# Sixteen modulation tiles of a hybrid layer: from split products on 128 stationary columns to plain fp32 products on four column groups

## The chip, the core and the metric

The kernel runs on one core of a Trainium2 chip. The metric is the device time of one execution in microseconds (us): the median of several runs, and, for the reading, one execution recorded by the hardware profiler.

## What is computed

One layer of a diffusion backbone works on 1280 tokens (1024 latent, 256 context) of width 1024 in fp32: norm, modulation, one input projection, attention beside a bidirectional scan, output projection, feed-forward. The part that matters here is the modulation (adaLN):

```python
def adaln(cond, w_mod, b_mod):
    m = jax.nn.silu(cond) @ w_mod + b_mod      # cond: 1024 values, w_mod: 1024 x 6144
    return jnp.split(m, 6, axis=-1)            # shift, scale, gate (mixer), shift, scale, gate (FFN)
```

It is called for two vectors, `c` (latent tokens) and `c_ctx` (context tokens), with the same `w_mod`. So it is a product of a 2 x 1024 matrix with a 1024 x 6144 matrix: much weight, and only two rows of result.

## The kernel before, in words

`w_mod` is cut into 24 tiles of 256 columns (`MOD_W`), each 1024 x 256: 1 MB, held as 128 partitions x 8 k-pieces x 256. The first eight (`FirstMod`, L229) are computed at the start, while the first data arrive, and are not touched by the change. The other sixteen (`ModStage`, L307), numbered n = 0 to 15 here (tile 8 + n of the 24), run between the tiles of the input projection.

**Numbers.** Nearly all products of the kernel are "split" ones: a value is written as hi + lo, both in the format fp32r, and TensorE multiplies hi by hi, hi by lo and lo by hi (`split3`, L407; lines L409 to L411 of the profile are these three for all such products). For a modulation tile ScalarE copies the tile rounded into `hi` (`act_hi`, L342, 128 x 2048 elements), VectorE subtracts to get `lo` (`dve_lo`, L348). The stationary operand `cond_st` has 128 columns: 32 copies of hi and 32 of lo of the first vector, then the same of the second. The product (`pe_product`, L354) is 16 matmuls for one tile: 8 k-pieces, each with `hi` and with `lo` as the moving operand of 256 columns, all added up in one PSUM tile of 128 x 256, `psM`. VectorE copies `psM` into `row` (`dve_row`, L366). Then `pe_turn` (L373) multiplies with a 0/1 matrix of two columns, `K_SUM`, that adds row 0 and row 32 of each half. For a gate tile (n = 0 to 3 and 12 to 15) the 0/1 matrix is the stationary operand (2 columns) and the moving one has 256 columns (L380); for the other eight the row is stationary (128 columns, two of them) and the moving operand has 2 columns (L383). Both are in plain fp32. `dve_col` (L387) takes the result out of PSUM, and GpSimd's queue stores the gate rows.

**Order.** `SEQUENCE` (L52) is the hand-written order of the input projection: 14 projection tiles with smaller steps (fold, cache, sums) among them. A projection tile is 72 split matmuls in three token blocks. `mod_step(n)` on TensorE is `pe_turn(n - 1)` and then `pe_product(n)`. `MODS` (L58) gives its places: n = 0 before the first smaller step, n = 1 to 6 each behind one projection tile, 7 to 14 two for each of the tiles 8 to 11 (one in the middle of the tile, one behind it), 15 in the middle of tile 12. On ScalarE and VectorE `act_hi` and `dve_lo` stand at places of the same list (`at_start`, `after`, `ahead`), among the splits of the projection weights, the convolutions of the xbc tiles and the evictions.

**Buffers.** The weight tiles go through a ring of two (`m2_wring`), loaded by SP's queue in order with the projection weights; the load of tile n waits until `dve_lo` of tile n - 2 is done (L337). `hi`, `lo` and `psM` have one slot each. Later the place of the ring and of `hi`/`lo` is used for the z weights: ScalarE's split of the first of these waits for the last `dve_lo` (L763), VectorE's for the last modulation product (L954).

Of the kernel before, what the change touches and what calls it, by code (L numbers as in the profile page):

```python
# [23 lines left out]
P = 128  # L24
F32 = mybir.dt.float32
# [7 lines left out]
KD = D // P  # L33
# [37 lines left out]
C_GPRE, C_GFFN, C_BMOD, C_GQ, C_GKV, C_CW, C_CB, C_GS, C_DB, C_AL, C_DS = 0, 8, 16, 64, 67, 69, 93, 101, 105, 121, 137  # L71
N_COLS = 141

K_ID, K_MASK, K_SEL, K_FOLD, K_TRI, K_SA, K_SB, K_MT, K_MD, K_SUM = 0, 128, 384, 400, 528, 656, 672, 672, 688, 704
N_CONST = 706


class Chain:
# [58 lines left out]
def across(ap, n):  # L137

    p, a = ap.shape
    return ap.unsqueeze(2).to_broadcast([p, a, n])  # L140
# [166 lines left out]
class ModStage:  # L307

    def __init__(self, L, st, tag, first, last, banks, depth, slots):
        self.L, self.first, self.last, self.banks, self.depth, self.slots = L, first, last, banks, depth, slots
        self.ring = L.sb(st, f"{tag}_wring", [P, depth, KD, MOD_W])
        self.hi, self.lo = (L.sb(st, f"{tag}_w_{n}", [P, slots, KD, MOD_W], F32R) for n in ("hi", "lo"))
        self.row = L.sb(st, f"{tag}_row", [P, MOD_W])
        self.gate = L.sb(st, f"{tag}_gate", [2, 2, MOD_W])
        self.psM = L.ps(st, f"{tag}_psM", [P, banks, 512])
        self.psC = L.ps(st, f"{tag}_psC", [P, 512])
        self.loaded = [L.sem(f"{tag}_w_loaded{i}") for i in range(depth)]  # L320
        self.row_out = [L.own_sem(f"{tag}_row_out{i}") for i in range(2)]
        self.hi_ready, self.lo_ready, self.product, self.row_ready, self.turned, self.col_ready = (
            L.sem(f"{tag}_{n}") for n in ("w_hi", "w_lo", "product", "row_ready", "turned", "col_ready"))

    @staticmethod
    def is_gate(j):
# [6 lines left out]
    def load(self, eng, j):  # L333
        i = j - self.first
        r = i % self.depth
        if i >= self.depth:
            eng.wait_ge(self.lo_ready, i + 1 - self.depth)  # L337
        eng.dma_start(flat(self.ring[:, r, :, :]), self.L.dram["w_mod"][j]).then_inc(self.loaded[r], 16)

    def act_hi(self, act, j):  # L340
        i = j - self.first
        r = i % self.depth  # L342
        act.wait_ge(self.loaded[r], 16 * (i // self.depth + 1))
        if i >= self.slots:
            act.wait_ge(self.product, i + 1 - self.slots)
        act.activation(self.hi[:, i % self.slots, :, :], self.ring[:, r, :, :], ACT.Copy).then_inc(self.hi_ready, 1)

    def dve_lo(self, dve, j):  # L348
        i = j - self.first
        dve.wait_ge(self.hi_ready, i + 1)  # L350
        dve.tensor_tensor(self.lo[:, i % self.slots, :, :], self.ring[:, i % self.depth, :, :],
                          self.hi[:, i % self.slots, :, :].bitcast(F32), ALU.subtract).then_inc(self.lo_ready, 1)

    def pe_product(self, pe, j):  # L354
        i = j - self.first
        pe.wait_ge(self.lo_ready, i + 1)
        if i >= self.banks:
            pe.wait_ge(self.row_ready, i + 1 - self.banks)
        for k in range(KD):
            for w in (self.hi, self.lo):  # L360
                mm = pe.matmul(self.psM[:, i % self.banks, :MOD_W], self.L.cond_st[:, k, :],
                               w[:, i % self.slots, k, :], start=(k == 0 and w is self.hi),
                               stop=(k == KD - 1 and w is self.lo))
        mm.then_inc(self.product, 1)

    def dve_row(self, dve, j):  # L366
# [6 lines left out]
    def pe_turn(self, pe, j):  # L373
        i = j - self.first
        pe.wait_ge(self.row_ready, i + 1)
        if i >= 1:
            pe.wait_ge(self.col_ready, i)
        total = self.L.const[:, K_SUM:K_SUM + 2]
        if self.is_gate(j):
            mm = pe.matmul(self.psC[0:2, :MOD_W], total, self.row[:], start=True, stop=True)  # L380
        else:
            for s in range(2):
                mm = pe.matmul(self.psC[:, 2 * s:2 * s + 2], self.row[:, s * P:(s + 1) * P], total, start=True,  # L383
                               stop=True)
        mm.then_inc(self.turned, 1)
# [36 lines left out]
def phase_front(L):  # L422
# [6 lines left out]
    with ExitStack() as st:  # L429
# [19 lines left out]
        def at(name, home, skip, shape, dt=F32):  # L449
# [37 lines left out]
        staged = at("w_mod_staged", "hT_hi", 0, [P, 2, KD, T])  # L487
        spare_hi, spare_lo = (at(f"m1_w_{n}", "m2_wring", i * KD * MOD_W * 4, [P, KD, MOD_W], F32R)
                              for i, n in enumerate(("hi", "lo")))
        first_rows = at("m1_rows", "m2_row", 0, [P, 2, MOD_W])  # L490
        first = FirstMod(L, lambda k: staged[:, :, k, 0:KD // 2 * MOD_W], (mod.hi[:, 0, :, :], spare_hi[:]),
                         (mod.lo[:, 0, :, :], spare_lo[:]), (mod.psM[:, 0, :], psP[:, 0, 1, :]), mod.psC, first_rows)
# [61 lines left out]
        after = lambda m: MODS.get(number.get(m), ())[len(midway(m)):]  # L554
        splits = lambda m: SPLIT_AT.get(number.get(m), ())
        for_tile = lambda ct: ct < N_TILES

        def ahead(m):

            return midway(m + 1 + (SEQUENCE[m + 1][0] == "sumq")) if m + 1 < len(SEQUENCE) else ()  # L560

        def at_start(m):

            before = [i for i in range(m) if SEQUENCE[i][0] == "xbc" and ahead(i) == midway(m)]
            return () if before else midway(m)


        down = list(range(NT_LAT - 1, -1, -1)) + list(range(NT - 1, NT_LAT - 1, -1))
# [187 lines left out]
        def _(act):  # L756
            chain = Chain(act, ach)

            def split(ct):
                act.wait_ge(loaded[ct % 2], 16 * (ct // 2 + 1))  # L760
                if not for_tile(ct):
                    n = ct - N_TILES
                    act.wait_ge(mod.lo_ready, last_mod)  # L763
                    act.activation(flat(wz_hi[:, 2 * n:2 * n + 2, :]), flat(raw[:, ct % 2, :, :]), ACT.Copy
                                   ).then_inc(hi_ready, 1)
                    return
                if ct >= 2:
                    until(act, tiles[ct - 2])
                act.activation(w_hi[:, ct % 2, :, :], raw[:, ct % 2, :, :], ACT.Copy).then_inc(hi_ready, 1)
# [15 lines left out]
            for n in range(3 * KD):  # L785
# [2 lines left out]
                    split(1)  # L788
                if n in X_LATER:
                    norm.act_square(act, X_LATER[n])  # L790
            mod.act_hi(act, MOD_EARLY)
            act.wait_ge(ip_consts, 3)
            for m, (kind, i) in enumerate(SEQUENCE):
                for ct in splits(m)[:1]:
                    split(ct)
                for n in at_start(m):
                    mod.act_hi(act, MOD_EARLY + n)
                for ct in splits(m)[1:]:
                    split(ct)
                for n in after(m):  # L800
                    if n >= 1:
                        mod.act_hi(act, MOD_EARLY + n)
                src = flat(bank(m))[:, 0:T]
                if kind == "rope":
                    until(act, m)
# [1 line left out]
                    act.activation(conv[64:128, :], src[0:64, :], ACT.Copy).then_inc(swapped, 1)  # L807
                    act.activation(dt_raw[64:80, :], src[64:80, :], ACT.Copy).then_inc(dt_copied, 1)
                if kind == "xbc":
                    for n in ahead(m):  # L810
                        mod.act_hi(act, MOD_EARLY + n)
                    n = xbc_order.index(i)
                    act.wait_ge(conv_ready, n + 1)
                    if i >= 6:
                        act.wait_ge(kv_stored, 16)
                        until(act, place["out", 0])
                    elif i == 0:
                        until(act, place["sumq", 0])
                    elif i == 2:
                        act.wait_ge(qn_ready, KQ)  # L820
                    elif i == 3:
                        act.wait_ge(q_stored, 16)
                    act.activation(L.xbcT[:, i, :], conv[:], ACT.Silu,
                                   bias=L.cols[:, C_CB + i:C_CB + i + 1]).then_inc(conv_read, 1)
                    continue
# [121 lines left out]
        def _(dve):  # L947
# [101 lines left out]
            for n in range(3 * KD):  # L1049
# [5 lines left out]
                    norm.dve_mean(dve, X_LATER[n])  # L1055
                if n - 1 in X_LATER:
                    norm.dve_scale(dve, X_LATER[n - 1])
            mod.dve_lo(dve, MOD_EARLY)
            dve.wait_ge(turn.h_ready, 24)
            for m, (kind, i) in enumerate(SEQUENCE):  # L1060
                for n in splits(m)[:1]:
                    split(n)
                for n in at_start(m):
                    mod.dve_lo(dve, MOD_EARLY + n)
                for n in midway(m):
                    mod.dve_col(dve, MOD_EARLY + columns(m)[0])
                    mod.dve_row(dve, MOD_EARLY + n)
                for n in splits(m)[1:]:
                    split(n)
                for n in after(m):  # L1070
                    if n >= 1:
                        mod.dve_lo(dve, MOD_EARLY + n)
                src = flat(bank(m))
                if kind == "rope":
                    dve.wait_ge(t_loaded, 32)
# [53 lines left out]
                for n in columns(m)[-1:]:  # L1129
                    mod.dve_col(dve, MOD_EARLY + n)  # L1130
                if kind == "xbc":
                    for n in ahead(m):
                        mod.dve_lo(dve, MOD_EARLY + n)
                    if SEQUENCE[m - 1][0] == "sumq":
                        normalise(KQ, 3, C_GQ, qn_ready)
                if kind == "kv" and i == 1:
# [86 lines left out]
        def _(pe):  # L1223
# [54 lines left out]
            for n in range(2 * KD - 2, 3 * KD):  # L1278
                first_tiles(n, (1,))
            pe.wait_ge(turn.modulated, 3 * KD)  # L1280
            mod_step(0)
            for m, (kind, i) in enumerate(SEQUENCE):
                if m < 2:
# [1962 lines left out]
def shape_constants(np):  # L3246
# [8 lines left out]
    const[:, K_FOLD:K_FOLD + P] = (i % 64) == (j % 64)  # L3255
    const[:, K_TRI:K_TRI + P] = i <= j
    const[:, K_SUM:K_SUM + 2] = (i % 32 == 0) & (i // 64 == np.arange(2)[None, :])
    forward = np.arange(16) < SH
    const[:, K_SA:K_SA + 16] = np.where(forward, 1.0, -1.0)
    const[:, K_SB:K_SB + 16] = np.where(forward, 0.0, 1.0)  # L3260
# [92 lines left out]
```

## Time and profile before

| | |
|---|---|
| median of 3 runs | 1720.67 us (1719.91 to 1720.94) |
| profiled execution, first to last instruction (span) | 1720.2 us |
| TensorE (PE) busy | 1661.6 us, 97% |
| VectorE (DVE) busy | 1041.4 us, 61% |
| ScalarE (ACT) busy | 726.0 us, 42% |
| granted TensorE clock, mean | 0.993 of full |

The profiled execution is known by its span alone; its own time beside it is not listed. Its span lies 0.5 us under the median of the runs and inside their range. In the timeline views each row is one instruction (or several of the same kind in sequence, with their count): start in us, length in us, engine, line, operation, output <- inputs, rows*columns of the stationary operand and the shape of the moving one; in brackets the idle time of the engine before it and what ended it. Matmuls are pipelined, so their lengths overlap: the time that one takes from the engine is the distance to the next start, not its length. PEld is the load of the stationary operand, which runs ahead of the matmul. DVEq is an event on VectorE's queue that comes with no work of its own.

### The profile page before, as it was taken

The page shows a single profiled execution, that of the slowest core. Times are in us where ns is not written, and L with a number is a line of the kernel's source. Part 1 is how long each engine was busy: PE and PEld are TensorE (multiplying, and loading weights), DVE is VectorE, ACT ScalarE, POOL GpSimd, SP SyncE. Part 2 cuts the span into 40 slices and gives each one's busy share as a digit, 9 for nine tenths or more (in the row PEclk, how much of TensorE's full clock was granted, in tenths as well). Part 3 has the DMA queues.
Part 4 walks back from the last instruction along what each step waited for, and adds up shares of the span by engine and source line. Part 5 has one row for each costly group of instructions (what it writes and reads, how often), then busy time and mean ns, then how long its engine had stood idle before and what let it go on. Part 6 is the DMA issues. An engine that isn't in the chain of part 4 may idle for free. (4 is left out here: it accounts for less than half of the span.)

```text
span 1720.2 us, 24950 instructions
## 1 busy us (share of the span) xinstructions
PE 1661.6 (97%) x9786; PEld 1488.8 (87%) x9795; DVE 1041.4 (61%) x1590; ACT 726.0 (42%) x1213; POOL 79.7 (5%) x116
## 2 busy tenths in 40 slices
PE   5999999999899999999999999999999999999998
PEld 5788888878778888887888999999999999888886
DVE  5856765338765555474578554555455545467788
ACT  5753332334544544464565333333333333434453
POOL 0110000014200000000100000000000000000011
PEclk9999999999999999999999999999999999999999
DMA  9234342012400000114321221222222224773455
GB/s 372 80 135 145 117 146 89 11 34 65 114 13 19 1 14 1 69 37 157 131 86 50 103 103 72 88 95 96 88 79 103 92 83 163 247 231 98 124 164 186
DMA packets 76292, 176.35 MB, mean 103 GB/s; under 512 B 10353, under 2 KB 26945, under 8 KB 74129
## 3 DMA queue, kind: packets, MB, share of 16 engines
q1 hardware_dynamic: 72080, 169.75, 28.6%
q0 software_dynamic: 4096, 5.01, 0.9%
q8 instruction: 79, 1.29, 0.3%
q14 instruction: 37, 0.30, 0.1%
HBM read 131.02 MB, written 43.70 MB: 102 GB/s over the span
## 5 line engine op out<-in xcount | busy, mean ns | idle before, releaser
L409 PE MATMUL psF<-gv,gu_ring 128*128 128x320 f32 x1224 | 379.3, 310 | 3.8 <-DVE gv L2714 3.1
L411 PE MATMUL psF<-gv,gu_ring 128*128 128x320 f32 x1224 | 378.9, 310 | 0.0
L410 PE MATMUL psF<-gv,gu_ring 128*128 128x320 f32 x1224 | 378.8, 310 | 0.0
L409 PEld LDWEIGHTS psF<-gv,gu_ring 128*128 128x128 f32 x1224 | 230.4, 188 | 4.7 <-issue 3.6
L410 PEld LDWEIGHTS psF<-gv,gu_ring 128*128 128x128 f32 x1224 | 230.4, 188 | 0.0
L411 PEld LDWEIGHTS psF<-gv,gu_ring 128*128 128x128 f32 x1224 | 230.4, 188 | 0.0
L409 PE MATMUL psF<-d_w_ring,d_hid_ring 128*128 128x512 f32 x360 | 140.2, 389 | 0.0
L410 PE MATMUL psF<-d_w_ring,d_hid_ring 128*128 128x512 f32 x360 | 140.1, 389 | 0.0
L411 PE MATMUL psF<-d_w_ring,d_hid_ring 128*128 128x512 f32 x360 | 140.1, 389 | 0.0
L409 PE MATMUL psP<-hT_hi,win_hi 128*128 128x512 f32 (+1 forms) x336 | 122.2, 364 | 2.3 <-DVE hT_lo L184 1.6
L2514 ACT ACTIVATE hraw<-psF 128x320 f32<-128x320 f32 x130 | 56.7, 438 | 149.8 <-PE psF L411 148.5
L411 PE MATMUL psP<-hT_hi,win_lo 128*128 128x512 f32 (+1 forms) x336 | 119.3, 355 | 0.0
L410 PE MATMUL psP<-hT_lo,win_hi 128*128 128x512 f32 (+1 forms) x336 | 119.2, 355 | 0.0
L2764 DVE TENSOR_TENSOR hraw<-hraw,psF 128x320 f32<-128x320 f32 x132 | 63.4, 485 | 41.1 <-ACT hraw L2514 35.1
L1843 DVE TENSOR_TENSOR pt_lo<-psPT,pt_hi 128x512 fp32r<-128x512 f32 (+1 forms) x104 | 58.3, 582 | 41.0 <-ACT pt_hi L1719 41.0
L2556 ACT ACTIVATE d_hid_ring<-d_hid 128x640 fp32r<-128x640 f32 x54 | 40.0, 740 | 98.5 <-PE psF L411 95.4
L2510 ACT ACTIVATE gu_ring<-raw_gu 128x512 fp32r<-128x512 f32 x65 | 40.9, 629 | 96.1 <-PE psF L411 96.1
L409 PEld LDWEIGHTS psF<-d_w_ring,d_hid_ring 128*128 128x128 f32 x360 | 67.6, 188 | 14.5 <-DVE hraw L2953 0.5
L411 PEld LDWEIGHTS psF<-d_w_ring,d_hid_ring 128*128 128x128 f32 x360 | 67.6, 188 | 14.1
L410 PEld LDWEIGHTS psF<-d_w_ring,d_hid_ring 128*128 128x128 f32 x360 | 67.6, 188 | 13.8
L2821 DVE TENSOR_TENSOR d_hid_ring<-d_hid,d_hid_ring 128x640 fp32r<-128x640 f32 x54 | 44.5, 824 | 53.8 <-ACT d_hid_ring L2556 53.6
L1719 ACT ACTIVATE pt_hi<-psPT 128x512 fp32r<-128x512 f32 (+1 forms) x104 | 52.2, 515 | 54.8 <-PE psPT L1985 53.6
(447 smaller groups left out, 3640.5 us busy)
## 6 DMA issues: line engine op xcount, KB each, us to landing
hid_variants<-hraw SPq DMA_DIRECT2D x77, 320.0 KB, 2.2
d_hid<-hid_variants SPq DMA_DIRECT2D x58, 320.0 KB, 3.0
m_wring<-in_w_mod SPq DMA_DIRECT2D x16, 1024.0 KB, 4.9
d_b<-in_w_down SPq DMA_DIRECT2D x44, 256.0 KB, 4.2
win_raw<-in_w_in SPq DMA_DIRECT2D x18, 512.0 KB, 5.4
w_mod_staged<-in_w_mod SPq DMA_DIRECT2D x16, 512.0 KB, 11.8
d_hid_more<-hid_variants SPq DMA_DIRECT2D x19, 320.0 KB, 3.0
raw_gu<-in_w_gate SPq DMA_DIRECT2D x11, 512.0 KB, 3.8
```

The costliest lines, as they stand in the source:

```text
L409: pe.matmul(out, w_hi, x_hi, start=first, stop=False, skip_group_check=onto)
L410: pe.matmul(out, w_hi, x_lo, start=False, stop=False, skip_group_check=onto)
L411: return pe.matmul(out, w_lo, x_hi, start=False, stop=last, skip_group_check=onto)
L1719: act.activation(pt_hi[:, g[0]:g[-1] + 1, r:r + P], psPT[:, (g0 + i) % 2, 0:len(g), :], ACT.Copy).then_inc(pth_ready, 1)
L1843: dve.tensor_tensor(pt_lo[:, g[0]:g[-1] + 1, r:r + P], psPT[:, (g0 + i) % 2, 0:len(g), :], pt_hi[:, g[0]:g[-1] + 1, r:r + P].bitcast(F32), ...
L2510: act.activation(w_slot(q)[:, 0, :], block_of(r, n), ACT.Copy).then_inc(wv_hi, 1)
L2514: act.activation(dst[:, chunk(c)], psA(n, c), ACT.Copy).then_inc(copied, 1)
L2556: act.activation(ring_h(e, 0), hr[e % HR], ACT.Copy).then_inc(h_hi, 1)
L2764: dve.tensor_tensor(dst[:, chunk(c)], src[:, chunk(c)], bank(c), ALU.add).then_inc(added, 1)
L2821: dve.tensor_tensor(ring_h(e, 1), hr[e % HR], ring_h(e, 0).bitcast(F32), ALU.subtract).then_inc(h_lo, 1)
```

## The change

The product of each of the sixteen tiles is taken in plain fp32, straight from the loaded tile. A new stationary operand, `cond_q`, has 32 columns for each k-piece: 16 copies of the first vector and 16 of the second. The eight k-pieces go in two rounds of four; the four of a round write four different quarters of the partitions of `psM` (0-31, 32-63, 64-95, 96-127), that is the four column groups of the array, and the second round adds onto them. The turn then adds four rows instead of two, with another 0/1 matrix of the same shape, `K_SUM4`. `act_hi` and `dve_lo` of the sixteen tiles go away, with their places in the order. The ring's load waits for the product instead of `dve_lo`, the product waits for the load itself, and ScalarE's first z split waits for the last product instead of the last `dve_lo`. VectorE makes `cond_q` once, at the place of the first `dve_lo`, behind a wait for the last of the first eight products, and TensorE waits for it before n = 0.

```diff
-K_ID, K_MASK, K_SEL, K_FOLD, K_TRI, K_SA, K_SB, K_MT, K_MD, K_SUM = 0, 128, 384, 400, 528, 656, 672, 672, 688, 704
-N_CONST = 706
+K_ID, K_MASK, K_SEL, K_FOLD, K_TRI, K_SA, K_SB, K_MT, K_MD, K_SUM, K_SUM4 = 0, 128, 384, 400, 528, 656, 672, 672, 688, 704, 706
+N_CONST = 708
...
 class ModStage:
+    QUARTER = P // 4
...
     def load(self, eng, j):
...
         if i >= self.depth:
-            eng.wait_ge(self.lo_ready, i + 1 - self.depth)
+            eng.wait_ge(self.product, i + 1 - self.depth)
         eng.dma_start(flat(self.ring[:, r, :, :]), self.L.dram["w_mod"][j]).then_inc(self.loaded[r], 16)
 
-    def act_hi(self, act, j):
...
-    def dve_lo(self, dve, j):
...
     def pe_product(self, pe, j):
         i = j - self.first
-        pe.wait_ge(self.lo_ready, i + 1)
+        r = i % self.depth
+        pe.wait_ge(self.loaded[r], 16 * (i // self.depth + 1))
         if i >= self.banks:
             pe.wait_ge(self.row_ready, i + 1 - self.banks)
-        for k in range(KD):
-            for w in (self.hi, self.lo):
-                mm = pe.matmul(self.psM[:, i % self.banks, :MOD_W], self.L.cond_st[:, k, :],
-                               w[:, i % self.slots, k, :], start=(k == 0 and w is self.hi),
-                               stop=(k == KD - 1 and w is self.lo))
+        for first in (0, 4):
+            for q in range(4):
+                mm = pe.matmul(self.psM[self.QUARTER * q:self.QUARTER * (q + 1), i % self.banks, :MOD_W],
+                               self.L.cond_q[:, first + q, :], self.ring[:, r, first + q, :], start=(first == 0),
+                               stop=(first == 4))
         mm.then_inc(self.product, 1)
...
-        total = self.L.const[:, K_SUM:K_SUM + 2]
+        total = self.L.const[:, K_SUM4:K_SUM4 + 2]
...
+        L.cond_q = at("cond_q", "m2_w_lo", 0, [P, KD, P // 4])
...
-                    act.wait_ge(mod.lo_ready, last_mod)
+                    act.wait_ge(mod.product, last_mod)
...
-            mod.act_hi(act, MOD_EARLY)
             act.wait_ge(ip_consts, 3)
             for m, (kind, i) in enumerate(SEQUENCE):
-                for ct in splits(m)[:1]:
+                for ct in splits(m):
                     split(ct)
-                for n in at_start(m):
-                    mod.act_hi(act, MOD_EARLY + n)
...
-            mod.dve_lo(dve, MOD_EARLY)
+            dve.wait_ge(first.product, KD)
+            dve.tensor_copy(L.cond_q[:].rearrange("p k (g r) -> p (k g) r", g=2), across(scond[:], P // 8)
+                            ).then_inc(cond_ready, 1)
             dve.wait_ge(turn.h_ready, 24)
...
-                    for n in ahead(m):
-                        mod.dve_lo(dve, MOD_EARLY + n)
...
             pe.wait_ge(turn.modulated, 3 * KD)
+            pe.wait_ge(cond_ready, 6)
             mod_step(0)
...
+    const[:, K_SUM4:K_SUM4 + 2] = i % 32 == 16 * np.arange(2)[None, :]
```

## Rows read from the trace of the kernel before

**Rows 1.** The page, busy time of each engine over the span

```profile
PE 1661.6 (97%) x9786; PEld 1488.8 (87%) x9795; DVE 1041.4 (61%) x1590; ACT 726.0 (42%) x1213; POOL 79.7 (5%) x116
```

**Rows 2.** The longest of PE's waits between 60 and 310 us (total, times, longest)

```profile
PE m_psM L361 <- DVE m_w_lo L351: 1.2, 1, 1.2
PE psP L409 <- DVEq L1126: 0.7, 1, 0.7
...
```

**Rows 3.** Instructions on the weight ring: count, min/median/max ns, first and last start

```profile
L346 ACT ACTIVATE m_w_hi<-m_wring x16: 1898/1916/1920, 77.7 to 272.9; 128x2048 fp32r<-128x2048 f32 x16
L351 DVE TENSOR_TENSOR m_w_lo<-m_wring,m_w_hi x16: 2270/2285/2294, 79.6 to 276.2; 128x2048 fp32r<-128x2048 f32 x16
```

**Rows 4.** PE's timeline around product 3, behind a gate turn

```profile
139.76 0.28 PE L411 MATMUL psP<-hT_hi,win_lo 128*128 128x256 f32 x1
139.97 0.59 PE L380 MATMUL m_psC<-m_row,const 128*2 128x256 f32 x2
140.50 0.39 PE L361 MATMUL m_psM<-m_w_hi,cond_st 128*128 128x256 f32 x1
140.72 0.28 PE L361 MATMUL m_psM<-m_w_lo,cond_st 128*128 128x256 f32 x1
...
142.49 0.39 PE L409 MATMUL psP<-hT_hi,win_hi 128*128 128x512 f32 x1
```

**Rows 5.** PE's timeline around product 5, behind a turn that is no gate

```profile
175.04 0.50 PE L383 MATMUL m_psC<-const,m_row 128*128 128x2 f32 x4
175.40 0.36 PE L361 MATMUL m_psM<-m_w_hi,cond_st 128*128 128x256 f32 x1
...
177.38 1.02 PE L1319 MATMUL psP<-xbcT,ones 128*128 128x512 f32 x2
```

**Rows 6.** Instructions of line L380: count, min/median/max ns

```profile
L380 PEld LDWEIGHTS m_psC<-m_row,const x16: 80/82/83, 102.5 to 289.2; 128*2 128x2 f32 x16
L380 PE MATMUL m_psC<-m_row,const x16: 377/378/378, 102.5 to 289.4; 128*2 128x256 f32 x16
```

**Rows 7.** PE's and PEld's timelines around the last turn, with no product behind it

```profile
288.95 0.28 PE L411 MATMUL psP<-hT_hi,win_lo 128*128 128x256 f32 x1
289.16 0.59 PE L380 MATMUL m_psC<-m_row,const 128*2 128x256 f32 x2
289.68 0.50 PE L409 MATMUL psP<-hT_hi,win_hi 128*128 128x512 f32 x1
...
289.16 0.09 PEld L380 LDWEIGHTS m_psC<-m_row,const 128*2 128x2 f32 x2
289.68 0.19 PEld L409 LDWEIGHTS psP<-hT_hi,win_hi 128*128 128x128 f32 x1 [0.44 <-issue]
```

**Rows 8.** PE's timeline: first product and next step, xbc tile, product 6 and next

```profile
83.35 0.28 PE L361 MATMUL m_psM<-m_w_hi,cond_st 128*128 128x256 f32 x1
...
85.68 0.79 PE L1293 MATMUL m_psC<-const,xbcT 16*128 16x16 f32 x10 [0.28 <-DVEq L1082]
...
180.42 0.51 PE L409 MATMUL psP<-hT_hi,win_hi 128*128 128x512 f32 x1 [0.73 <-DVEq L1126]
...
194.28 0.50 PE L383 MATMUL m_psC<-const,m_row 128*128 128x2 f32 x4
196.01 0.39 PE L361 MATMUL m_psM<-m_w_hi,cond_st 128*128 128x256 f32 x1 [1.23 <-DVE m_w_lo L351]
...
198.01 0.39 PE L409 MATMUL psP<-hT_hi,win_hi 128*128 128x512 f32 x1
```

**Rows 9.** VectorE's work: making `cond_st` (mean ns of one)

```profile
L1034 DVE CAST cond_st<-cond_hi 128x512 fp32r<-128x512 f32 x1 | 0.4, 426 | 0.0
```

**Rows 10.** DMA issues of 40 to 310 us: count, KB each, us to landing

```profile
m_wring<-in_w_mod SPq DMA_DIRECT2D x16, 1024.0 KB, 4.9
```

**Rows 11.** ACT's and DVE's timelines: first z split, and last z split

```profile
278.54 1.06 ACT L764 ACTIVATE wz_hi<-win_raw 128x1024 fp32r<-128x1024 f32 x1 [0.95 <-DVE m_w_lo L351]
...
302.43 1.23 DVE L955 TENSOR_TENSOR wz_lo<-win_raw,wz_hi 128x1024 fp32r<-128x1024 f32 x1 [3.39 <-ACT wz_hi L764]
```

More of the change, by code:

```diff
@@ L321, in __init__ @@
         self.row_out = [L.own_sem(f"{tag}_row_out{i}") for i in range(2)]
-        self.hi_ready, self.lo_ready, self.product, self.row_ready, self.turned, self.col_ready = (
-            L.sem(f"{tag}_{n}") for n in ("w_hi", "w_lo", "product", "row_ready", "turned", "col_ready"))
+        self.product, self.row_ready, self.turned, self.col_ready = (
+            L.sem(f"{tag}_{n}") for n in ("product", "row_ready", "turned", "col_ready"))
     @staticmethod
@@ L336, in load, with pe_product @@
         if i >= self.depth:
-            eng.wait_ge(self.lo_ready, i + 1 - self.depth)
+            eng.wait_ge(self.product, i + 1 - self.depth)
         eng.dma_start(flat(self.ring[:, r, :, :]), self.L.dram["w_mod"][j]).then_inc(self.loaded[r], 16)
-    def act_hi(self, act, j):
+    def pe_product(self, pe, j):
         i = j - self.first
         r = i % self.depth
[L343 to L346, printed above, removed]
-    def dve_lo(self, dve, j):
[L349 to L355, printed above, removed]
-        pe.wait_ge(self.lo_ready, i + 1)
+        pe.wait_ge(self.loaded[r], 16 * (i // self.depth + 1))
         if i >= self.banks:
             pe.wait_ge(self.row_ready, i + 1 - self.banks)
-        for k in range(KD):
-            for w in (self.hi, self.lo):
-                mm = pe.matmul(self.psM[:, i % self.banks, :MOD_W], self.L.cond_st[:, k, :],
-                               w[:, i % self.slots, k, :], start=(k == 0 and w is self.hi),
-                               stop=(k == KD - 1 and w is self.lo))
+        for first in (0, 4):
[3 more added lines that the diff above has]
+                               stop=(first == 4))
         mm.then_inc(self.product, 1)
@@ L556, in phase_front @@
         for_tile = lambda ct: ct < N_TILES
[L558 to L565, printed above, removed]
         down = list(range(NT_LAT - 1, -1, -1)) + list(range(NT - 1, NT_LAT - 1, -1))
@@ L790, in _ @@
                     norm.act_square(act, X_LATER[n])
-            mod.act_hi(act, MOD_EARLY)
             act.wait_ge(ip_consts, 3)
             for m, (kind, i) in enumerate(SEQUENCE):
-                for ct in splits(m)[:1]:
+                for ct in splits(m):
                     split(ct)
-                for n in at_start(m):
-                    mod.act_hi(act, MOD_EARLY + n)
[L798 to L802, printed above, removed]
                 src = flat(bank(m))[:, 0:T]
@@ L809, in _ @@
                 if kind == "xbc":
-                    for n in ahead(m):
-                        mod.act_hi(act, MOD_EARLY + n)
                     n = xbc_order.index(i)
@@ L1062, in _ @@
                     split(n)
-                for n in at_start(m):
-                    mod.dve_lo(dve, MOD_EARLY + n)
                 for n in midway(m):
@@ L1069, in _ @@
                     split(n)
-                for n in after(m):
-                    if n >= 1:
-                        mod.dve_lo(dve, MOD_EARLY + n)
                 src = flat(bank(m))
@@ L1131, in _ @@
                 if kind == "xbc":
-                    for n in ahead(m):
-                        mod.dve_lo(dve, MOD_EARLY + n)
                     if SEQUENCE[m - 1][0] == "sumq":
```

## The prediction

> **What bounds the kernel now.** I read the page's engine line first: TensorE is busy for 97% of the span, VectorE 61%, ScalarE 42% [rows 1]. That average says nothing of the stretch in which the change lies, so next come the waits of PE from 60 to 310 us. There are four, the longest 1.2 and 0.7 us, 2.4 us in all [rows 2]. Through the whole input projection, then, PE's own instruction stream sets the time: what the change does to PE's stream is what it does to the end, and what it takes from other engines counts only where PE waited for them. Last I read PE's timeline around single modulation steps for the distance from start to start.
>
> **The splits that go.** Sixteen ScalarE copies of 1.92 us (31 us) and sixteen VectorE subtractions of 2.29 us (37 us) [rows 3] are removed. Nearly all of it was hidden behind PE. What PE waited for is one subtraction: product 6 starts behind a wait of 1.23 us. From the turn's start to the next step that place takes 198.01 - 194.28 = 3.73 us [rows 8], where the same step elsewhere takes 177.38 - 175.04 = 2.34 us [rows 5]. So 1.39 us goes. The wait of 0.73 us on the convolution at 180.42 [rows 8] stays: VectorE had been idle before that convolution, and what is late next is the same convolution. That gives product 5, ahead of it, a cushion of 0.73 us either way. Product 0 has one too: it fills 83.35 to 85.25, and PE waits until 85.68 anyway [rows 8].
>
> **The products, old.** An old product is 16 matmuls, one every (142.49 - 140.72)/15 = 0.118 us [rows 4], 1.9 us in all. With its turn the step takes 2.34 us where the turn is no gate [rows 5]. Behind a gate turn it is 142.49 less 139.88 (the start of the last matmul before it, and 0.12 for that): 2.61 us [rows 4]. Seven products stand behind a gate turn (n = 1 to 4, 13 to 15), eight behind the other kind (5 to 12), n = 0 behind none.
>
> **The products, new.** No row shows an fp32 matmul on a quarter of the columns beside another, so I build it from the gate turn, the only fp32 product here with a few stationary columns. The eight gate turns leave 16 records [rows 6]: one fp32 matmul is two records, each with a load of its own. The pair lasts 0.59 us with records of 0.378 us [rows 4, 6], so the second starts 0.21 us behind the first. A new product is 8 such matmuls, 16 records of 0.213 us. What they cost depends on which run side by side.
>
> Records of PE start in the order of the program in all the rows. A matmul's second record writes the same columns as its first, so it can't start before the first has streamed; the next group's first record stands behind it and can go with it. Then two records run at any time: 8 x 0.213 + 0.213 = 1.92 us for a product, as much as the old one. I take this value, because it follows from the order that every row shows and from the pair that rows 4 show. The ends are 4 x 0.213 = 0.85 us, if all four groups run at once, and 16 x 0.213 = 3.41 us, if none does.
>
> The Trainium skill bears on this order. Its page "TensorE: Matmul & The Clock Gate", section "Part 3: Packing small matmuls — row/col tiling", says that matmuls are strictly in order in start and end and only weight loads are pulled ahead; by that rule the sum is the 1.92 us just taken, and it speaks against a gain here. No run so far shows two column groups at work.
>
> Changing to narrow columns and back has a price in the rows. The last turn starts 0.09 us late (289.16 against 288.95 + 0.12). Its two records stream until 289.16 + 0.43 = 289.59; the next matmul starts at 289.68 and is 0.11 us longer than the usual 0.39, with its load not ahead of it: 0.20 us more [rows 4, 7]. Zero is one bound (the loads run ahead), twice this the other.
>
> **The sum.** Behind a turn that is no gate: 0.36 (turn) + 0.09 + 1.92 + 0.20 = 2.57 us against 2.34, +0.23 each. Seven of them are +1.6 us; product 5 goes into its cushion. Behind a gate turn, which is narrow itself, the change is paid once as before: 0.09 + 0.43 + 1.92 + 0.20 = 2.64 against 2.61, +0.03 by seven, +0.2 us. Product 0 ends at 83.35 + 2.21 = 85.56, inside its cushion. With the wait that goes: 1.6 + 0.2 - 1.4 = +0.4 us. On the span of 1720.2 us that is 1720.6; the median of the runs lies 0.5 us above the span, so 1721 us.
>
> **Edits at no cost, and their cover.** Making `cond_q`: 256 columns on VectorE, at most the 0.43 us of a 512-column cast of the same kind [rows 9], in place of a 2.29 us subtraction. The turn's other 0/1 matrix has the same shape. The ring's load of tile n now waits for product n - 2 instead of its subtraction. It is issued later, but product n is still a whole projection tile (16 us or more) behind product n - 2, and a load lands in 4.9 us [rows 10]. Behind it in SP's queue stand the projection weights, which are needed more than a tile later; if that cover failed, PE would stand for what is left of the 4.9 us, once for each tile. ScalarE's first z split, at 278.5 now [rows 11], moves to the last product at 283.4. Behind it on ScalarE is only the activation of a projection tile that ends at 289; VectorE's half, which already waited for that product, comes perhaps 0.2 us later. The chain of the last z weights ends at 303.7 [rows 11] and starts from the end of that tile, not from the moved split.
>
> **The rivals.** (1) All four groups overlap. Then a product streams for 0.85 us: 0.36 + 0.09 + 0.85 + 0.20 = 1.50 against 2.34, -0.84 by seven; 1.57 against 2.61, -1.04 by seven; products 0 and 5 give nothing, since PE waits behind them. With the 1.4: -14.6 us, 1706. For it: the two loads of the narrow turn start together within 0.09 us [rows 7], so a record's load does not wait for the one before. Against: the order of starts. The Trainium skill's page "TensorEngine Tiling (Array Packing)", section "Theoretical Speedup", gives up to 4 for a dimension of 32 or less, which is this case.
>
> (2) The loads are exposed. The first load of each new group waits until the record before has started, and its 0.08 to 0.11 us [rows 4, 6] lies bare: some 0.10 us for each of seven group changes. A product is then 2.62 us and a step +0.93 by seven (+0.20 for product 5), +0.73 by seven, +0.6 for product 0: 6.5 + 0.2 + 5.1 + 0.6 - 1.4 = +11 us, 1732. It decides from about 0.03 us of bare load per group change on: fourteen products by seven changes by 0.03 are 3 us, which with the 0.4 of the sum is 0.2% of the time. For it: behind the narrow turn the next load did come late [rows 7]. Against: that load was for the full width. The Trainium skill's page "TensorE: Matmul & The Clock Gate", in the same section, lets loads overlap running matmuls only if the row group differs, and these groups share all rows; by that rule it is this case.
>
> (3) The groups do not overlap at all, so the change doesn't do what it is written for. A product is 3.41 us: +1.72 by seven, +1.0 for product 5 past its cushion, +1.52 by seven, +1.4 for product 0, less 1.4: +23.6 us, 1744. The change of width that the narrow turn pays [rows 7] speaks against it: the array does seem to be set to a quarter.
>
> **How the numbers follow.** About 0.2% (3.4 us) is what a measurement of this kernel can tell from no change. My forecast (two records at a time) has 0.36, four at a time 0.27, exposed loads 0.19, no overlap 0.18. With the change of width at zero the forecast's own sum is 15 x 0.29 less, 1717; at twice, 1726: so 0.03 of its 0.36 is faster, 0.27 the same, 0.06 slower. Faster: 0.27 + 0.03 = 0.30. Same: 0.27. Slower: 0.06 + 0.19 + 0.18 = 0.43. Faster and slower cases hold most of the chance, so the range must span both: from 1703, a little under rival 1 for a cheaper change of width, to 1735, a little over rival 2; it leaves out rival 3 with 0.18. The forecast's own range is 1717 to 1726. The predicted time is that of the forecast, 1721 us.
>
> **What would show it.** In the changed kernel's PE timeline, between two modulation steps: 16 records of about 0.38 us per product; starts in pairs, a group's first record together with the second of the group before, and 1.9 us from the first record to the end of the last stream. Four starts within 0.05 us are rival 1, gaps of 0.1 us at each new group rival 2, even starts every 0.21 us rival 3. The waits of PE should show no subtraction, and no DMA on the weight ring: one of those would prove the cover of the loads wrong. The 0.73 us wait on the convolution should shrink by what product 5 grows. ScalarE should lose 31 us and VectorE 37 us of busy time without the span following.

## The result and the profile after

The changed kernel takes 1707.23 us (median of 4 runs, 1706.29 to 1709.75) against 1720.74 us (median of 4) of the kernel before: a ratio of 0.9923 [0.9911, 0.9936], 13.5 us faster. The forecast was no change at 1721 us; the result lies in the range and within 1.3 us of rival 1 (all four column groups at once, 1706 us). The profiled execution, the slowest of the four, took 1709.75 us, with a span of 1707.9.

The page of the changed kernel, busy time of each engine, answers to [rows 1]:

```profile
PE 1650.0 (97%) x9795; PEld 1469.3 (86%) x9795; DVE 1006.6 (59%) x1575; ACT 696.4 (41%) x1197; POOL 79.6 (5%) x116
```

VectorE lost 34.8 us and ScalarE 29.6 us of busy time. The span became 12.3 us shorter; the table below finds 13.0 us between product 0 and the last turn, in TensorE's stream. TensorE's share is again 97%. Whether four groups overlapped can be seen only in the timeline, so that comes next.

The instructions on the new product's tile (count, min/median/max ns, first and last start):

```profile
L348 PEld LDWEIGHTS m_psM<-m_wring,cond_q x256: 106/109/110, 83.6 to 270.0; 128*32 128x32 f32 x128
L348 PE MATMUL m_psM<-m_wring,cond_q x256: 379/379/403, 83.6 to 270.2; 128*32 128x256 f32 x128
```

Each of the 16 products is 16 records of 0.379 us; at the prediction's distance of 0.213 us, with no overlap between groups, they would stream for 3.41 us. PE's timeline of the changed kernel at product 0, asked for in windows that end at 83.7, 83.85 and 84.3 us. A line folds the records that start inside the window; `x` counts them:

```profile
83.60 0.42 PE L348 MATMUL m_psM<-m_wring,cond_q 128*32 128x256 f32 x4
...
83.60 0.63 PE L348 MATMUL m_psM<-m_wring,cond_q 128*32 128x256 f32 x7
...
83.60 1.07 PE L348 MATMUL m_psM<-m_wring,cond_q 128*32 128x256 f32 x16
```

Four records start within 0.42 - 0.38 = 0.04 us (records that start together are logged as 0.38 to 0.40 us long), and 0.21 us later the next ones. The product is over 1.07 us after its first start; the forecast had 1.92.

PE's timelines around product 3 (behind a gate turn) and products 5 and 6 (behind the other turn), which answer to [rows 4, 5, 8]:

```profile
137.49 0.28 PE L398 MATMUL psP<-hT_hi,win_lo 128*128 128x256 f32 x1
137.70 0.38 PE L367 MATMUL m_psC<-m_row,const 128*2 128x256 f32 x1
137.71 0.42 PE L348 MATMUL m_psM<-m_wring,cond_q 128*32 128x256 f32 x3
137.91 0.38 PE L367 MATMUL m_psC<-m_row,const 128*2 128x256 f32 x1
137.95 1.20 PE L348 MATMUL m_psM<-m_wring,cond_q 128*32 128x256 f32 x13
139.08 0.50 PE L396 MATMUL psP<-hT_hi,win_hi 128*128 128x512 f32 x1
...
170.35 0.50 PE L370 MATMUL m_psC<-const,m_row 128*128 128x2 f32 x4
170.78 1.07 PE L348 MATMUL m_psM<-m_wring,cond_q 128*32 128x256 f32 x16
171.79 2.42 PE L1284 MATMUL psP<-xbcT,ones 128*128 128x512 f32 x6
176.10 0.50 PE L396 MATMUL psP<-hT_hi,win_hi 128*128 128x512 f32 x1 [1.90 <-DVEq L1092]
...
191.59 0.50 PE L370 MATMUL m_psC<-const,m_row 128*128 128x2 f32 x4
192.03 1.07 PE L348 MATMUL m_psM<-m_wring,cond_q 128*32 128x256 f32 x16
193.03 0.50 PE L396 MATMUL psP<-hT_hi,win_hi 128*128 128x512 f32 x1
```

The lines of 137.71 and 137.91 decide the order of starts. In the program the turn's two records stand ahead of all product records; here three records of the product start 0.20 us ahead of the turn's second. That they are those of the three groups that the turn, which sits in the first group, leaves free is inferred: the trace does not name the groups.

The signal that a product is done did not run ahead, though. It hangs on the last matmul in the program, and VectorE's copy of the tile waits for it:

```profile
139.24 0.42 DVE L358 COPY m_row<-m_psM 128x256 f32<-128x256 f32 x1 [0.79 <-PE m_psM L348]
```

In the trace the record that carries this signal starts at 138.39 us and, by its length of 0.38, is over at 138.77, while the last record of the product runs until 137.95 + 1.20 = 139.15. The copy starts at 139.24, behind that one. So it is at all seven products behind a gate turn: records pass each other at their starts, and the one signal of the product came only when all of them were done.

Where the 13 us come from, read from turn to turn in PE's timeline of both kernels (us, first start to next first start; rival 1's figure is the prediction's):

| stretch | before | after | difference | rival 1 |
|---|---|---|---|---|
| product 0 to turn 0 | 19.17 | 18.81 | -0.36 | 0 |
| turns 0 to 4, four steps behind a gate turn | 72.52 | 67.94 | -4.58 | -4.2 |
| turn 4 to turn 5 | 19.24 | 21.24 | +2.00 | 0 |
| turn 5 to turn 6 (product 6, with the split's wait) | 11.94 | 9.75 | -2.19 | -2.2 |
| turns 6 to 12, six other steps | 55.64 | 50.83 | -4.81 | -5.0 |
| turns 12 to 15, three behind a gate turn | 27.30 | 24.24 | -3.06 | -3.1 |
| sum | 205.81 | 192.81 | -13.00 | -14.6 |

The waits of PE from 60 to 310 us in the changed kernel, against [rows 2]:

```profile
PE psP L396 <- DVEq L1092: 1.9, 1, 1.9
PE m_psC L1258 <- DVEq L1048: 0.9, 1, 0.9
```

No wait on a subtraction is left, and none on the weight ring's DMA. The wait on the convolution has grown from 0.73 to 1.90 us, which is 1.17 of the +2.00 in the table. The rest is in the table of short stretches behind that wait. The columns are: stretch, length, busy time (and count) of PE, PEld, DVE, ACT and POOL, granted clock, DMA share, GB/s.

```profile
176.00:178.00 2.00, 1.90 (x5) 1.52 (x6) 0.49 (x2) 1.98 (x2) 0.00 (x0) 0.64 0.64 260
178.00:180.00 2.00, 2.00 (x6) 1.56 (x5) 0.35 (x1) 1.99 (x3) 0.00 (x0) 0.51 0.00 0
180.00:182.00 2.00, 2.00 (x10) 1.62 (x10) 2.00 (x1) 1.85 (x2) 0.00 (x0) 1.00 0.00 0
```

Behind the wait the granted clock is 0.51, that is the level of 1.2 GHz, for some 3 us: 6 matmuls in 2 us where 10 follow at 1.00. The projection tile from the wait's end to the next turn takes 191.59 - 176.10 = 15.49 us, where it took 194.28 - 180.42 = 13.86: +1.63. From turn 4 to the start of the wait PE took (180.42 - 0.73) - 175.04 = 4.65 us before and (176.10 - 1.90) - 170.35 = 3.85 after, so product 5 gave 0.80. That closes the account: 1.17 + 1.63 - 0.80 = 2.00.

The wait thus took 0.37 us more than product 5 gave. VectorE's rows for the last part of the convolution, before and after:

```profile
178.53 1.67 DVE L1122 SCALAR_TENSOR_TENSOR conv_acc<-psP,cols,conv_acc 128x1023 f32<-128x1023 f32 x2
...
173.85 1.67 DVE L1088 SCALAR_TENSOR_TENSOR conv_acc<-psP,cols,conv_acc 128x1023 f32<-128x1023 f32 x2
```

The convolution ends 5.16 us behind turn 4 before and 5.17 us after, so it is not later. PE goes on 0.22 us behind its end before (180.42 - 180.20) and 0.58 us after (176.10 - 175.52). What held up VectorE's event in between is not settled.

### The profile page after: what moved, and what is told of

Read it like the earlier page. It is cut to its first block and busy times, and to the rows that moved or that the text cites. A ratio compares the mean times of both kernels' runs of the same rounds, so it can differ in the third digit from the quotient of the medians.

```text
span 1707.9 us, 24911 instructions
## 1 busy us (share of the span) xinstructions
PE 1650.0 (97%) x9795; PEld 1469.3 (86%) x9795; DVE 1006.6 (59%) x1575; ACT 696.4 (41%) x1197; POOL 79.6 (5%) x116
## 5 line engine op out<-in xcount | busy, mean ns | idle before, releaser
L396 PEld LDWEIGHTS psP<-hT_hi,win_hi 128*128 128x128 f32 x336 | 64.2, 191 | 18.3 <-issue 4.6
```

Source lines behind the costliest of these rows:

```text
L396: pe.matmul(out, w_hi, x_hi, start=first, stop=False, skip_group_check=onto)
```

## The experiments

Eight more kernels ran: the changed kernel again, and seven with an edit to it. The first four below ran on one chip beside the kernel before at 1721.1 us (median of 13), the other four on another beside 1721.03 us (median of 11); each ratio is to the kernel before on the same chip.

**One group.** All eight matmuls of a product accumulate in the first 32 columns, and the turn's 0/1 matrix takes those rows alone.

```diff
-        for first in (0, 4):
-            for q in range(4):
-                mm = pe.matmul(self.psM[self.QUARTER * q:self.QUARTER * (q + 1), i % self.banks, :MOD_W],
-                               self.L.cond_q[:, first + q, :], self.ring[:, r, first + q, :], start=(first == 0),
-                               stop=(first == 4))
+        for k in range(KD):
+            q = k % 1
+            mm = pe.matmul(self.psM[self.QUARTER * q:self.QUARTER * (q + 1), i % self.banks, :MOD_W],
+                           self.L.cond_q[:, k, :], self.ring[:, r, k, :], start=(k < 1), stop=(k >= KD - 1))
```

> All eight matmuls of a product go to the first column group; nothing else changes. Theory (the gain is four groups streaming at once): a product streams 16 x 0.213 = 3.41 us instead of 0.85, +2.56 us for each of 14 products; products 0 and 5 lose part of it to the waits of 0.90 and 1.90 us behind them (+1.7, +0.7), and the half clock behind the second wait (1.6 us) goes: about +36 us on the changed kernel, some 1744 us. Rival (the gain is the 68 us of split work taken off ScalarE and VectorE): that work stays away here, so about 1707 us, at most a few us more.

Measured: 1744.13 us (1743.68 to 1744.59), ratio 1.0134 [1.0107, 1.0161], 23 us slower than the kernel before. PE's timeline, at product 7:

```profile
201.91 3.64 PE L348 MATMUL m_psM<-m_wring,cond_q 128*32 128x256 f32 x16
205.48 0.50 PE L395 MATMUL psP<-hT_hi,win_hi 128*128 128x512 f32 x1
```

A product now streams for 3.64 us (15 x 0.213 + 0.38 = 3.58). The splits are gone here too, and it is slower: the gain is the overlap of the groups and not the work taken from VectorE and ScalarE.

**Two groups.** The same edit with `q = k % 2`, and `k < 2` and `k >= KD - 2` for start and stop.

> The eight matmuls go to two column groups in turn. Theory (each group streams its own records, groups at once): 8 x 0.213 = 1.71 us a product, +0.85 for 14 products, nothing for products 0 and 5, the half clock perhaps gone: +10 to +12 us, 1717 to 1719 us. Rival (two records at a time whatever the groups, by the order of starts): a product takes as long as with four groups, so 1707 us, unless four groups already beat that order. Rival (splits): 1707 us.

Measured: 1718.03 us (median of 8, 1714.27 to 1721.11), ratio 0.9981 [0.9969, 0.9994]. PE's timeline, product 5 and the wait behind it:

```profile
172.96 1.92 PE L348 MATMUL m_psM<-m_wring,cond_q 128*32 128x256 f32 x16
174.81 2.42 PE L1283 MATMUL psP<-xbcT,ones 128*128 128x512 f32 x6
178.29 0.50 PE L395 MATMUL psP<-hT_hi,win_hi 128*128 128x512 f32 x1 [1.06 <-DVEq L1091]
```

Two groups at a time give 1.92 us, the forecast's figure for a product. The rival of this run, that two records run at a time whatever the groups, would have left the time at 1707 us. So the size of a record was right, and what failed is only how many run side by side. The price falls with the number of groups: 3.64, 1.92 and 1.07 us for one, two and four.

**Group by group.** The same eight matmuls in four groups, with the two of a group one behind the other in the program.

```diff
-        for first in (0, 4):
-            for q in range(4):
+        for q in range(4):
+            for first in (0, 4):
```

> The same eight matmuls, but both of a group right behind each other, so four records of one group stand in the program ahead of the next group's first. Theory A (each group has a line of its own and is fed far ahead): no change, products of 1.07 us, 1707 us. Theory B (starts follow the program, two at a time): a new group starts every 0.64 us, 4 x 0.64 + 0.21 = 2.8 us a product, +1.9 for 14 products, +27 us, 1734 us. In between (fed a few records ahead): products of 1.3 to 2 us, 1710 to 1720 us.

Measured: 1704.87 us (1704.23 to 1705.51), ratio 0.9906 [0.9879, 0.9933], an interval that overlaps the changed kernel's. PE's timeline of product 3, in windows that end at 136.0 and at 137.0, then PEld's of the first product, up to 81.4:

```profile
135.48 0.59 PE L367 MATMUL m_psC<-m_row,const 128*2 128x256 f32 x2
135.91 0.43 PE L348 MATMUL m_psM<-m_wring,cond_q 128*32 128x256 f32 x4
...
135.91 1.08 PE L348 MATMUL m_psM<-m_wring,cond_q 128*32 128x256 f32 x16
...
81.25 0.18 PEld L348 LDWEIGHTS m_psM<-m_wring,cond_q 128*32 128x32 f32 x8
```

If starts went in program order, four records of one group would stand in a row and hold up the next group. Yet four records start within 0.05 us, and the whole takes 1.08 us. The fourth group's first record stands 12 records behind the first group's. So inside a product the order of the matmuls in the program hardly matters (1.08 us against 1.07): each group has a line of its own.

Behind a gate turn the order does show. There the product starts behind both records of the turn (135.91 against 135.48), unlike at 137.71 in the changed kernel, and turns 0 to 4 take 68.16 us in place of 67.94. In the program five records of the first group (the turn's second and four of the product) stand here between the turn's first and the next group's first; in the changed kernel there are three, and those were passed. How far ahead a group is fed was not tried further.

**Splits back, unread.** The changed kernel's product, and besides it the sixteen ScalarE copies and VectorE subtractions at their old places with their old waits; nothing reads what they write.

```diff
+            eng.wait_ge(self.lo_ready, i + 1 - self.depth)
...
+        act.activation(self.hi[:, i % self.slots, :, :], self.ring[:, r, :, :], ACT.Copy).then_inc(self.hi_ready, 1)
...
+        dve.tensor_tensor(self.hi[:, i % self.slots, :, :], self.ring[:, i % self.depth, :, :],
+                          self.hi[:, i % self.slots, :, :].bitcast(F32), ALU.subtract).then_inc(self.lo_ready, 1)
```

> The changed product, with ScalarE's copy and VectorE's subtraction of all sixteen tiles put back at their old places and with their old waits; nobody reads what they write (the subtraction writes over the copy). Theory (the splits were hidden but for one): product 6 waits again for what is ahead of it on VectorE, +1.4 us, and the load of the ring goes as before: 1708 to 1710 us. Rival (the gain came from the splits): back to about 1720 us.

Measured: 1707.26 us (median of 4, 1704.53 to 1707.89), ratio 0.9921 [0.99, 0.9942]. The grouped lines of ScalarE and VectorE, 60 to 310 us, PE's timeline at product 6, and a wait of PE between turns 2 and 3:

```profile
L348 ACT ACTIVATE m_w_hi<-m_wring 128x2048 fp32r<-128x2048 f32 x16 | 30.6, 1912 | 43.5 <-PE m_psM L364 34.5 <-DVE m_w_hi L353 9.0
...
L353 DVE TENSOR_TENSOR m_w_hi<-m_wring,m_w_hi 128x2048 fp32r<-128x2048 f32 x16 | 36.6, 2286 | 6.3 <-ACT m_w_hi L348 6.2
...
188.99 0.50 PE L386 MATMUL m_psC<-const,m_row 128*128 128x2 f32 x4
189.42 1.07 PE L364 MATMUL m_psM<-m_wring,cond_q 128*32 128x256 f32 x16
190.42 0.50 PE L412 MATMUL psP<-hT_hi,win_hi 128*128 128x512 f32 x1
...
144.37 0.38 PE L1239 MATMUL m_psC<-const,conv_acc 128*64 128x128 f32 x2 [0.63 <-DVE xbcT L1031]
```

30.6 + 36.6 = 67 us of work are back, and the time is the changed kernel's within the spread of the runs: nearly all of that work lay beside TensorE. The 1.4 us expected at product 6 did not come: here the product reads the ring itself, does not wait for the subtraction, and its step is 1.43 us as in the changed kernel (1.44).

Not all of it is hidden, though. Product 0 to turn 0 takes 19.10 us (18.81 in the changed kernel), and turns 0 to 4 take 68.91 (67.94), with the wait of 0.63 us on a copy that VectorE makes right behind a subtraction. Against this the stretch from turn 4 to turn 5 takes 19.28 in place of 21.24, since no half clock came in this execution. Without the 1.63 us of the half clock the changed kernel would take 191.18 us from product 0 to turn 15; with the splits back it is 192.11. So about 0.9 of the 67 us reached TensorE.

**The changed kernel again, and filler work in front of the wait.** The second adds 14 matmuls of 256 columns behind product 5, into columns that nobody reads, so that TensorE is busy for most of the 1.9 us in which it otherwise waits.

```diff
+        if i == 5:
+            for k in range(14):
+                mm = pe.matmul(self.psM[:, 0, MOD_W:2 * MOD_W], self.L.hT_lo[:, k % KD, 0:P],
+                               self.L.hT_hi[:, k % KD, 0:MOD_W], start=True, stop=True)
```

> The changed kernel once more, as the base of the next three. 1705 to 1708 us. Theory (the half clock behind the 1.90 us wait comes in some executions only): its profile has the wait of 1.9 us at the xbc tile behind the sums whether the clock falls or not.

> Fourteen matmuls whose result nobody reads are added to product 5, 14 x 0.118 = 1.65 us, ahead of the wait of 1.90 us for the convolution. Theory (that wait is slack on PE, and PE standing still in it is what lets the clock fall): the wait shrinks to about 0.25 us, the clock stays full behind it, and the time is the same as the changed kernel's or up to 1.6 us less. Rival (the wait is not fixed by VectorE's convolution, or the clock falls for another reason): 1.6 us more, or half clock again.

Measured: 1706.75 us (median of 6, 1704.03 to 1711.31), ratio 0.9921 [0.9905, 0.9937], for the changed kernel; 1706.33 us (median of 5, 1704.8 to 1708.12), ratio 0.9916 [0.9902, 0.9929], with the filler. The wait in PE's timeline and the stretch behind it, of the changed kernel run again, of the one with filler, and of group by group from above (columns of the stretches as before):

```profile
177.59 0.50 PE L396 MATMUL psP<-hT_hi,win_hi 128*128 128x512 f32 x1 [1.90 <-DVEq L1092]
...
178.00:180.00 2.00, 2.00 (x7) 1.50 (x6) 0.20 (x2) 1.97 (x3) 0.00 (x0) 0.52 0.43 176
```

```profile
175.69 0.50 PE L400 MATMUL psP<-hT_hi,win_hi 128*128 128x512 f32 x1 [0.24 <-DVEq L1096]
...
176.00:178.00 2.00, 2.00 (x10) 1.63 (x9) 0.30 (x2) 1.97 (x3) 0.00 (x0) 1.00 0.98 401
```

```profile
173.99 0.50 PE L396 MATMUL psP<-hT_hi,win_hi 128*128 128x512 f32 x1 [1.89 <-DVEq L1092]
...
174.00:176.00 2.00, 2.00 (x9) 1.65 (x10) 0.49 (x2) 1.98 (x2) 0.00 (x0) 1.00 0.66 266
```

The changed kernel shows the half clock behind its wait for the second time. With filler the wait is 0.24 us and the clock stays at 1.00. But group by group has the same wait (1.89 us) and no half clock behind it, so such a wait is not always followed by a fall, and one profile with filler does not show that the filler prevented it. The 1.6 us of a fall are less than the runs of one kernel differ by (7 us here), and the medians, 0.4 us apart, do not tell whether filling the wait pays. That stays open. Part of what the runs differ by lies ahead of the change: in the eight profiles with the same first stage (the kernel before, the changed kernel twice, and the five edits up to here) product 0 starts at 81.3 to 85.1 us.

**The first eight tiles too.** The same product for the first stage, which the change left as it was: its splits, the conditioning's own split and the old stationary tile are left out.

```diff
-        pe.wait_ge(self.lo_ready, k + 2 if k >= 1 else 1)
+        if k >= 1:
+            pe.wait_ge(self.loaded[k], 32)
+        else:
+            pe.wait_ge(self.half_loaded, 16)
...
-            for w in (self.hi, self.lo):
-                mm = pe.matmul(self.banks[k % 2][:, :MOD_W], self.L.cond_st[:, i, :], w[k % 2][:, i, :],
-                               start=(i == 0 and w is self.hi), stop=(i == KD - 1 and w is self.lo))
+            for q in range(4):
+                mm = pe.matmul(self.banks[k % 2][32 * q:32 * (q + 1), :MOD_W], self.L.cond_q[:, 4 * h + q, :],
+                               self.raw(k)[:, h, q * MOD_W:(q + 1) * MOD_W], start=(h == 0), stop=(h == 1))
```

> The first eight modulation tiles are done the same way: plain fp32 in four column groups straight from the loaded tile, their sixteen splits and the split of the vector left out. Theory (here the splits do lie on the path: the last tile's copy of 1.9 us and subtraction of 2.3 us stand between its landing and its product): 3 to 6 us less than the changed kernel, 1701 to 1704 us. Rival (the start waits for the token loads that follow in the same queue, up to about 50 us): less than 1 us.

Measured: 1701.48 us (median of 4, 1700.31 to 1703.35), ratio 0.9888 [0.9874, 0.9903]: the fastest version, 5.3 us under the changed kernel on the same chip. The end of the first stage in the changed kernel (the last subtraction on VectorE, the last product's last matmul on PE), and then, of this kernel, PE's timeline with the last two products of the stage, PE's longest waits up to 60 us, the start of product 0 of the later stage (in a window that ends at 78.4 us), and four matmuls of the projection on either side of 42.65 us:

```profile
35.92 2.29 DVE L264 TENSOR_TENSOR m_w_lo<-w_mod_staged,m_w_hi 128x2048 fp32r<-128x2048 f32 x1 [0.75 <-ACT m_w_hi L258]
...
41.03 0.27 PE L276 MATMUL psP<-m_w_lo,cond_st 128*128 128x256 f32 x1
```

```profile
31.53 1.93 PE L261 MATMUL m_psM<-w_mod_staged,cond_q 128*32 128x256 f32 x16 [3.55 <-DMA w_mod_staged<-in_w_mod]
34.33 1.93 PE L261 MATMUL psP<-w_mod_staged,cond_q 128*32 128x256 f32 x16
...
PE m_psM L261 <- DMA w_mod_staged<-in_w_mod: 10.4, 5, 4.8
...
78.03 0.64 PE L333 MATMUL m_psM<-m_wring,cond_q 128*32 128x256 f32 x8
...
40.88 0.63 PE L382 MATMUL psP<-hT_lo,win_hi 128*128 128x512 f32 x1
41.30 0.63 PE L383 MATMUL psP<-hT_hi,win_lo 128*128 128x512 f32 x1
...
43.09 0.40 PE L382 MATMUL psP<-hT_lo,win_hi 128*128 128x512 f32 x1
43.33 0.39 PE L383 MATMUL psP<-hT_hi,win_lo 128*128 128x512 f32 x1
```

PE now waits for the transfer itself. In the changed kernel the last tile went through a copy and then the subtraction, over at 38.2 us, before its product could run until 41.3; here the last product is over at 34.33 + 1.93 = 36.3 us, 5.0 us earlier. Product 0 of the later stage starts at 78.03 us; in the eight profiles with the old first stage it starts at 81.3 to 85.1 (83.60 and 85.07 in the changed kernel), so it is 3 to 7 us earlier, and the 5.3 us between the medians fit that. In this stage the split work was on the path, since each tile of weights is waited for as it lands.

A product takes 1.93 us here in place of 1.07. This is the lower clock: the trace's record of the granted clock begins at 42.65 us in this execution, and up to there every matmul is spaced about twice as far, 41.30 - 40.88 = 0.42 us for 512 columns against 43.33 - 43.09 = 0.24 behind it. So TensorE ran this whole first stage, with waits of up to 4.8 us between its products, at the level of 1.2 GHz, and the gain came in spite of it. (A stretch without a clock record is printed as 1.00; that figure is no reading.)

**Both.** The first eight tiles too, and the filler of above, in one kernel.

> Both edits of the two runs before together. Theory: their gains add, 3 to 7 us less than the changed kernel. Rival: as the run with the first eight alone.

Measured: 1702.1 us (median of 4, 1701.16 to 1703.78), ratio 0.9894 [0.9877, 0.9911]. Without the filler it was 1701.48: no gain to be seen, and the rival holds. That version's own wait on the convolution (1.53 us) was followed by no half clock in its profile, so there was nothing for the filler to save.

## Why the prediction was wrong

**The step that failed** is the one on the new products: "Records of PE start in the order of the program in all the rows", and from it "Then two records run at any time". In the rows that it names each matmul lies in columns that the next one needs as well, so they could not show what separate groups do. The rows at 137.71 and 137.91 show records that start ahead of an earlier one, and the group-by-group kernel shows that inside a product each group keeps its own line, though four records of one group stand in a row in the program. The term "8 x 0.213 + 0.213 = 1.92 us for a product" measured 1.07 from the first start to the last end. Two groups, where two records do run at any time, took 1.92.

**The rule behind that order.** The Trainium skill's page "TensorE: Matmul & The Clock Gate", section "Part 3: Packing small matmuls — row/col tiling", has matmuls start and end strictly in order. The rows at 137.71 and 137.91 contradict this for the starts across column groups, so the measurement decides; the signal of the product, which came behind the last of its records (139.24 against 139.15), does keep to it. The section's rule on weight loads (overlap only where the row group differs) is not borne out either: eight loads of 0.109 us, in groups that share all rows, took 0.18 us in the PEld row above. The Trainium skill's page "TensorEngine Tiling (Array Packing)", section "Theoretical Speedup", gives up to 4 for this case. The runs show 3.64 / 1.07 = 3.4.

**What held of rival 1.** Its steps, worked out from the same rows as the forecast's, came out at -1.04 behind a gate turn (measured -1.09 on average of seven) and -0.84 behind the other (measured -0.80 over six). So the price of changing width and back (0.09 + 0.20) was right in size, as was the 0.213 us of a record. Its -1.4 for the split's wait was right: product 6's stretch gave 2.19 us where 1.4 + 0.84 = 2.24 was said.

**What was mis-sized in it.** The stretch from turn 4 to turn 5 was put at no change, since product 5's gain would go into the wait. It became 2.00 us longer: 0.37 us because the wait grew by more (1.17) than product 5 gave (0.80), and 1.63 us for the half clock behind it. Product 0, also put at nothing, gave 0.36; with the splits back it gave 0.07, so most of this came with the split work that was gone from VectorE, and not with the product. Together with the small differences this is the whole gap between -14.6 and the -13.0 of the stretch; the medians differ by 13.5. That the half clock was the effect of the longer wait is only argued: two executions have it, and one of another kernel has as long a wait without it.

**The covers** named in the prediction held. PE has no wait on the ring's loads. The first z split moved behind the last product, as said, and made nothing wait. The splits' 67 us were hidden but for what product 6 waited and some 0.9 us more, which the kernel with the splits back shows.

**Rivals 2 and 3.** The gaps of exposed loads are not there: four starts within 0.04 us. That the groups do not overlap is refuted as well; but its price was right, 1744 us forecast and 1744.13 measured for the kernel with one group, where a product streams for 3.64 us (3.41 said).

**The chances.** Nothing in the rows of before tells one line for the array from one line for each group. With 0.36 against 0.27 the forecast stood ahead by the weight of an order that had only been seen within one group. The range reached both, and held.

## What to carry to other kernels

Small stationary sides (32 columns) put in four column groups stream beside each other, and inside a product the matmuls of the groups need not be interleaved by hand; plain fp32 at its price of two records per matmul then costs less than a split into two products over the full width. Such a change is worth what TensorE's own stream loses, and the split work that goes with it is worth little (about 0.9 of 67 us here, and the one wait at product 6) unless TensorE waits for each tile as it lands. Before an order of starts is taken from a trace for a new case, ask whether any row has independent resources in it.

## What was not expected of the hardware

Records of one engine passed each other: three of a later matmul's started 0.20 us ahead of an earlier one's second. In the group-by-group kernel the record that starts with the first stands 12 records behind it in the program. Yet the signal of the whole product came behind the last of its records. Eight loads of 32 columns took 0.18 us together, where one alone is 0.109.

In two profiles of the changed kernel the clock fell to about half for some 3 us behind a wait of 1.90 us and cost 1.6 us; in the group-by-group kernel a wait of 1.89 us was followed by none.
